# A two-layer diffusion backbone on one core: adaLN weight tiles of 256 rows by 1024 columns, later mask loads, per-feature signals, gates in the down stage

## The chip, the core and the metric

One core of a Trainium2 chip runs the whole step as one program. The metric is the device time of one execution in microseconds (us). Before the change it is 1769.07 us, the median of three runs (1765.26, 1769.07 and 1769.55 us).

## What is computed

Two groups of 128 tokens (prompt and sample, D = 1024) go through two layers. Each layer has an adaLN modulation, a mixer and a channel mixer. Layer 0 has HGRN heads beside latent attention, then a dense SwiGLU of width 2816. Layer 1 has RWKV-7 time mixing, then eight experts.

```python
def modulation(cond, w, b):
    mod = jax.nn.silu(cond) @ w + b
    return [m[:, None, :] for m in jnp.split(mod, 6, axis=-1)]
...
        sh_m, sc_m, gt_m, sh_f, sc_f, gt_f = modulation(cond, ada_w[l], ada_b[l])
        h = rms_norm(x, norm_gains[l, 0]) * (1.0 + sc_m) + sh_m
...
        x = x + gt_m * rms_norm(out, norm_gains[l, 1])
        h = rms_norm(x, norm_gains[l, 2]) * (1.0 + sc_f) + sh_f
...
        x = x + gt_f * rms_norm(ff, norm_gains[l, 3])
```

## The kernel before

Everything is written by hand, engine by engine, with semaphores; the order of instructions in each block is the order on that engine. All large weights stream through `ring`, eleven slots of 1 MB (128 partitions by 2048 floats). SyncE issues the loads in the order of use (L429 to L540) and waits for `tile_used` before it fills a slot again. Small inputs come over ScalarE's own DMA queue (L1476 to L1489), a few over GpSimd's.

**adaLN.** Twelve groups `n` (six per layer: shift, scale and gate of the mixer, and of the channel mixer) each need a product of the conditions (two columns in `CT`) with 1024 by 1024 weights. A group is four ring tiles (`ada_group`, L450). In the kernel before a tile holds 256 output columns for all 1024 rows, as 1 KB runs, so `ada_part` (L649) on TensorE waits for all four tiles before its first matmul, and `tile_freed` (L107) gives none of the four slots back before the group's end. `take_sums` (L1563) on ScalarE copies a group's sums from PSUM, `turn_mods` (L660) turns them by TensorE, and `mods` (L1961) on VectorE makes shifts and scales of them.

**The start.** TensorE waits at L695 for `rows_in` (13 loads, the two token tiles X among them) and for the constants `cst_in`, turns the parameter rows, and VectorE and ScalarE make `CT`. ScalarE squares X, takes the root and scales it (`norm_x`, L1507). TensorE does groups 0 and 1, turns the normed tokens (`turn`, L682), and VectorE and ScalarE write the modulated features `HT` (`modulated`, L1926 and L1524; eight instructions of 128 features each, one signal `ht` at the end). Then `half` (L712) multiplies HT with the 12 tiles of the input projection, interleaved with the decay levels (`level`), for which VectorE needs the masks `MSK`, cast from the load `msk` by GpSimd (L554).

**Between the output projection and the SwiGLU.** TensorE multiplies four tiles of `ev_w_out` (`tile_product`, L635), then does groups 6 and 7, turns them and waits for the normed X. ScalarE copies each tile of the output into O (`take`, L1553), then squares all of O (`norm_o`, L1519), takes groups 6 and 7, and then squares X again (`norm_x(1)`). VectorE multiplies O by the gates (`gated`), adds to X (`residual`), makes `mods` 6 and 7, scales X and modulates. After HT, TensorE spreads the gate vector of the channel mixer over the tokens (`gates(1)`, L668: 16 matmuls into banks 4 to 7), ScalarE copies it to GB, and only then `hidden()` (L922) begins. It computes the SwiGLU by a seven-product scheme: `gate_up(j)` for 11 column blocks, then `down(n)` for 11 row blocks. VectorE prepares sums of weights (`up_sums`) and of features (`x_sums`, L2235 to L2241); `gate_up(0)` needs the first features for its first product and all of `x_sums` for its second (L953 to L955).

Of the kernel before, what the change touches and what calls it, by code (L numbers as in the profile page):

```python
# [28 lines left out]
P = 128  # L29
# [75 lines left out]


def tile_freed(m):  # L107

    for n, a in enumerate(ADA_FIRST):
        if a <= m < a + ADA_TILES:  # L110
            return ada_taken(n)
    return m + 1
# [62 lines left out]
def program(nc, t, out):  # L175
    ctx = ExitStack()
    with ctx:
# [90 lines left out]

        def turned_bank(n):
            return bank[(6, 7, 7, 7, 7, 7, 6, 7, 5, 6, 7, 7)[n]]  # L270
# [12 lines left out]
        EPS1, EPS2, SQ4 = SM[:, 192:193], SM[:, 193:194], SM[:, 194:198]  # L283
        XX = O[:, :, :].rearrange("p s (c n) -> p (s c) n", n=NST * P)
# [143 lines left out]
        def _(sp):  # L428
            walk = Walk()  # L429

            def tile(parts, i=None, per=0, dues=0):

                n = walk.n
                s, _ = walk.next(len(parts))
                if i is not None:
                    sp.wait_ge(sem("tile_used"), i * per + (n - RING + 1))
                    sp.wait_ge(sem("tile_used0"), i * per + (n - RING + 1))
                elif n >= RING:
                    sp.wait_ge(sem("tile_used"), tile_freed(tile_before(n)))
                for dst, src in parts:  # L440
                    sp.dma_start(dst(ring[:, s, :]), src).then_inc(sem(f"slot{s}"), 16)
# [102 lines left out]
        def _(pool):  # L544
# [20 lines left out]
            g.memset(KR[:, 0, 0:64], 0.0).then_inc(sem("kr_zero"), 1)  # L565
            g.memset(KR[:, 1, 0:64], 0.0).then_inc(sem("kr_zero"), 1)
            g.memset(KR[:, 2, 0:64], 0.0).then_inc(sem("kr_zero"), 1)
# [17 lines left out]
            pool.wait_ge(sem("tile_used"), tile_freed(N_V - RING))  # L585
# [17 lines left out]
        def _(pe):  # L603
# [43 lines left out]
            ada_tiles = []  # L647
# [47 lines left out]
            pe.wait_ge(sem("rows_in"), 16 * 13)  # L695
            pe.wait_ge(sem("cst_in"), 16)
# [12 lines left out]
            pe.wait_ge(sem("ht"), 2)  # L709
            held = {}  # L710

            def half(p, a):  # L712

                n = TW if EVEN_ORDER[p] < 11 else 160
                if a == 0:
                    held["w"] = arrived()[:, 0:KC * n].rearrange("p (k n) -> p k n", k=KC)
                    if p >= 2:
                        pe.wait_ge(sem("proj_copied"), p - 1)
                w, b = held["w"], bank[p % 2]
# [104 lines left out]
            pe.wait_ge(sem("kr_zero"), 3)  # L824
# [97 lines left out]
            def hidden():  # L922


                def gate_up(j):
# [42 lines left out]
                def down(n):  # L968
# [23 lines left out]
                    product(3, hs(3), w[:, 1, 1, :])  # L992

# [8 lines left out]
            pe.wait_ge(sem("ht"), 4)  # L1002
            gates(1)
            pe.wait_ge(sem("gb_copied"), 8)
# [37 lines left out]
            pe.wait_ge(sem("kk2"), 1)  # L1042
            for n in range(4):
                mm(target()[:, :], blk, W[6][:, n * 512:(n + 1) * 512], start=True, stop=True).then_inc(sem("proj_done"), 1)
# [282 lines left out]
            pe.wait_ge(sem("ht"), 8)  # L1327
# [139 lines left out]
        def _(act):  # L1467
# [8 lines left out]
            load(CST[:, :], t["cst"], "cst_in")  # L1476
# [10 lines left out]
            load(X[:, 0, :], t["x_prompt"][0], "rows_in")  # L1487
            load(X[:, 1, :], t["x_sample"][0], "rows_in")
            load(W[5][:, 0:MASKS * P], t["msk"], "msk_in")  # L1489
            act.wait_ge(sem("rows_in"), 16 * 13)  # L1490
            act.wait_ge(sem("pv"), 2)
# [5 lines left out]
            def load_root():  # L1497

                act.wait_ge(sem("eps"), 2)
                A(SM[:, 198:199], EPS1, ACT.Sqrt)  # L1500
# [22 lines left out]

            def modulated(k, scale, shift):  # L1524
# [9 lines left out]
                ins.then_inc(sem("ht"), 1)  # L1534

            def copy_gates(n):
                for k in range(4):
                    act.wait_ge(sem("gb_done"), 4 * n + k + 1)
                    A(GB[:, k // 2, (k % 2) * 512:(k % 2 + 1) * 512], bank[4 + k][:, :], ACT.Copy).then_inc(sem("gb_copied"), 1)  # L1539
# [30 lines left out]

            norm_x(0)
            for n in range(2):
                take_sums(n)
            modulated(0, 0, 0)
            def take_gates(p, dst):

                proj[0] += 1
                filled(N_EVEN_IN + p)
                at = slice(dst, dst + 512)
                A(FB[0][:, at], bank[p % 2][:, :], ACT.Sigmoid)  # L1580
                A(KG[:, at], bank[p % 2][:, :], ACT.Sigmoid, scale=-1.0).then_inc(sem("proj_copied"), 1)

            def take_even(p, dst, src, func=ACT.Copy):
                proj[0] += 1
                filled(N_EVEN_IN + p)
                A(dst, src(bank[p % 2]), func).then_inc(sem("proj_copied"), 1)
# [81 lines left out]
            load_root()  # L1668
            act.wait_ge(sem("down_done"), 1)
# [5 lines left out]
            sq[0] += 1  # L1675
            act.wait_ge(sem("meansq"), 1)
            A(SM[:, 4:6], SM[:, 2:4], ACT.Sqrt, scale=1.0 / D, bias=EPS1).then_inc(sem("root"), 1)
# [231 lines left out]
        def _(dve):  # L1909
# [16 lines left out]
            def modulated(k, scale, shift):  # L1926
# [9 lines left out]
                ins.then_inc(sem("ht"), 1)  # L1936
# [11 lines left out]
            def gated(n):  # L1948

                dve.wait_ge(sem("gb_copied"), 4 * (n + 1))  # L1950
                for st in range(NST):
                    v.tensor_tensor(TO[:, st, :], O[:, st, :], GB[:, st, :], ALU.mult).then_inc(sem("gated"), 1)

# [26 lines left out]
            v.memset(EPS1, EPS).then_inc(sem("eps"), 1)  # L1980
            v.memset(EPS2, 1e-12).then_inc(sem("eps"), 1)
# [4 lines left out]
            dve.wait_ge(sem("rows_in"), 16 * 13)  # L1986
# [6 lines left out]
            dve.wait_ge(sem("msk_bytes"), 1)  # L1993
            taken = [0]
# [237 lines left out]
            dve.wait_ge(sem("ht"), 4)  # L2232
# [98 lines left out]
            dve.wait_ge(sem("ht"), 6)  # L2331
# [393 lines left out]
```

## Time and profile before

| | before |
|---|---|
| median of the runs | 1769.07 us |
| profiled execution, its own time | 1767.48 us |
| its span in the profile | 1765.7 us |
| TensorE matmul busy | 1646.2 us (93%) |
| VectorE, ScalarE, GpSimd busy | 530.8, 299.8, 16.4 us |
| mean granted clock of TensorE | 0.971 |
| moved by DMA | 408.94 MB |

The trace counts from the span's start. A matmul of 32-bit floats appears as two records of MATMUL (PE) and of weight loads (PEld), so 32 records are 16 matmuls of the program. The chain of work is followed back from the last instruction; what lies on it decided the end. The granted clock is 1.00 at 2.4 GHz and 0.50 at 1.2 GHz.

### The profile page before, as it was taken

The numbers are of one execution on the slowest core, as the hardware profiler recorded it, in microseconds if no ns is written. First come the engines' busy times: TensorE is split into PE (matmuls) and PEld (weight loads), VectorE is DVE, ScalarE is ACT, GpSimd is POOL, SyncE is SP. The second block draws the span as 40 slices with busy tenths as digits, with TensorE's granted clock in tenths as the row PEclk, the third lists the DMA queues.
The fourth block names the chain that finished last, engine by engine and source line by source line (L and its number), as shares of the span: only waits on it lengthen the run. The fifth ranks groups of instructions, "written<-read, shape, count | busy, mean of one in ns | idle before, by whom it ended". The sixth has DMA issues, their size and how long they took to land.

```text
span 1765.7 us, 59234 instructions
## 1 busy us (share of the span) xinstructions
PE 1646.2 (93%) x27345; PEld 1469.7 (83%) x27345; DVE 530.8 (30%) x1253; ACT 299.8 (17%) x684; POOL 16.4 (1%) x32
## 2 busy tenths in 40 slices
PE   3999898999979999999498999999999999999996
PEld 1888477998447889889377999999999999999995
DVE  0363425767463446665614100000000101000001
ACT  1111413011023314333213001010101000010001
POOL 1000000000000000000000000000000000000000
PEclk9999998999999999999887999999999999999998
DMA  9722697545583320000524999999999999999880
GB/s 329 256 96 79 209 293 241 189 154 190 182 260 87 131 73 5 7 5 7 171 96 176 347 344 352 384 346 371 361 350 346 348 355 352 360 357 368 334 329 25
DMA packets 212032, 408.94 MB, mean 232 GB/s; under 512 B 13090, under 2 KB 135252, under 8 KB 211796
## 3 DMA queue, kind: packets, MB, share of 16 engines
q1 hardware_dynamic: 207344, 398.91, 63.9%
q8 instruction: 215, 3.52, 0.8%
q0 software_dynamic: 1184, 3.41, 0.7%
q10 hardware_dynamic: 3268, 2.93, 0.5%
q14 instruction: 21, 0.17, 0.0%
HBM read 403.30 MB, written 1.92 MB: 229 GB/s over the span
## 4 chain that ended last, share of the span: by engine, by line
PE 46%; PEld 42%; DVE 4%; issue 3%; ACT 2%; SPq 1%; DMA 1%; DVEq 0%; PEldq 0%; POOL 0%; ACTq 0%
PEld bank L1394 26%; PEld bank L1415 13%; PE bank L945 8%; PE bank L976 4%; PE bank L631 3%; PE bank L628 3%; PE bank L722 3%; PE bank L725 2%; PE bank L1155 2%; PE bank L1115 2%; PE bank L656 2%; PE bank L747 2%; PE bank L1151 2%; PE bank L1140 2%; PE bank L1091 2%
## 5 line engine op out<-in xcount | busy, mean ns | idle before, releaser
L1394 PEld LDWEIGHTS bank<-w,ring 128*64 128x64 f32 x11264 | 468.0, 137 | 19.4 <-issue 18.4
L1394 PE MATMUL bank<-w,ring 128*64 128x96 f32 x11264 | 476.7, 246 | 3.9 <-issue 3.2
L1415 PE MATMUL bank<-w,ring 128*64 128x96 f32 x5632 | 239.0, 246 | 2.8 <-issue 2.8
L1415 PEld LDWEIGHTS bank<-w,ring 128*64 128x64 f32 x5632 | 234.2, 137 | 5.9 <-issue 4.9
L2664 DVE TENSOR_TENSOR w<-w,bank 128x384 f32<-128x384 f32 (+1 forms) x48 | 23.6, 518 | 620.9 <-PE bank L1394 620.9
L1878 ACT ACTIVATE w<-bank 128x384 f32<-128x384 f32 (+1 forms) x48 | 20.5, 462 | 460.4 <-PE bank L1394 460.3
L656 PE MATMUL bank<-ring,ct 128*32 128x256 f32 x768 | 48.3, 405 | 16.0 <-DMA ring<-in_ada_w 14.4
L628 PE MATMUL bank<-w,ring 128*128 128x256 f32 x256 | 57.6, 387 | 5.8 <-DVE w L2342 5.2
L628 PEld LDWEIGHTS bank<-w,ring 128*128 128x128 f32 x256 | 49.4, 194 | 14.0 <-DVE w L2342 5.5
L631 PE MATMUL bank<-ring,w 128*128 128x256 f32 x256 | 58.1, 391 | 0.9 <-DVE w L1942 0.9
L631 PEld LDWEIGHTS bank<-ring,w 128*128 128x128 f32 x256 | 50.2, 197 | 8.5 <-DVE w L1942 1.3
L656 PEld LDWEIGHTS bank<-ring,ct 128*32 128x32 f32 x768 | 25.4, 116 | 35.8 <-issue 20.5
L2671 DVE SCALAR_TENSOR_TENSOR o<-bank,w,o 128x512 f32<-128x512 f32 x32 | 24.0, 751 | 90.0 <-PE bank L1376 88.0
L1155 PE MATMUL bank<-ht 64*64 64x64 f32 x1280 | 49.7, 219 | 0.0
L722 PE MATMUL bank<-ht,ring 128*128 128x256 f32 x192 | 45.3, 394 | 2.2 <-ACT ht L1532 2.2
L722 PEld LDWEIGHTS bank<-ht,ring 128*128 128x128 f32 x192 | 37.0, 196 | 8.3 <-ACT ht L1532 2.4
L1155 PEld LDWEIGHTS bank<-ht 64*64 64x64 f32 x1280 | 43.3, 135 | 0.5
L945 PE MATMUL bank<-ht,ring 128*128 128x128 f32 x352 | 43.0, 275 | 0.7 <-ACT gb L1539 0.7
L945 PE MATMUL bank<-w 128*128 128x128 f32 x352 | 42.9, 275 | 0.0
L945 PE MATMUL bank<-w,ring 128*128 128x128 f32 x352 | 42.9, 275 | 0.0
L725 PE MATMUL bank<-ring,ht 128*128 128x256 f32 (+1 forms) x192 | 41.9, 371 | 0.0
L945 PEld LDWEIGHTS bank<-ht,ring 128*128 128x128 f32 x352 | 41.1, 192 | 0.9 <-ACT gb L1539 0.9
(420 smaller groups left out, 1982.7 us busy)
## 6 DMA issues: line engine op xcount, KB each, us to landing
ring<-in_moe_w_gate SPq DMA_DIRECT2D x88, 1024.0 KB, 6.3
ring<-in_moe_w_up SPq DMA_DIRECT2D x88, 1024.0 KB, 6.5
ring<-in_moe_w_down SPq DMA_DIRECT2D x88, 1024.0 KB, 6.3
ring<-in_ada_w SPq DMA_DIRECT2D x48, 1024.0 KB, 6.2
ring<-in_ev_w_in SPq DMA_DIRECT2D x11, 1024.0 KB, 12.0
ring<-in_ffn_w_gate SPq DMA_DIRECT2D x11, 1024.0 KB, 7.7
ring<-in_ffn_w_up SPq DMA_DIRECT2D x11, 1024.0 KB, 5.6
ring<-in_ffn_w_down SPq DMA_DIRECT2D x11, 1024.0 KB, 6.5
```

The lines of the kernel that those rows point to most:

```text
L628: ins = mm(b[:, a * TW:(a + 1) * TW], w[:, k, a * P:(a + 1) * P], src[:, k, :], start=k == 0, stop=k == KC - 1)
L631: ins = mm(b[:, a * TW:a * TW + n], src[:, k, a * P:(a + 1) * P], w[:, k, 0:n], start=k == 0, stop=k == KC - 1)
L656: ins = mm(sums_bank(n)[32 * j:32 * j + 32, 0:TW], CT[:, NST * k:NST * k + 32], w[:, k, :], start=k == 0, stop=k == KC - 1)
L722: ins = mm(b[:, a * TW:(a + 1) * TW], w[:, k, a * P:(a + 1) * P], HT[:, k, :], start=k == 0, stop=k == KC - 1)
L725: ins = mm(b[:, a * TW:a * TW + n], HT[:, k, a * P:(a + 1) * P], w[:, k, 0:n], start=k == 0, stop=k == KC - 1)
L747: ins = mm(bank[2 + 2 * (n % 2) + h][:, j * P:(j + 1) * P], KG[hp, seg], WQ[hp, seg] if lv else W[0][hp, qs], start=True, stop=True)
L945: ins = mm(region(j, r)[:, which * P:(which + 1) * P], lhs(which, k), rhs(k), start=first and which == 0 and k == 0, stop=k == 3, skip_gro ...
L976: ins = mm(bank[DOWN_BANK[p]][:, :], lhs, rhs, start=n == 0, stop=n == FT - 1)
L1091: ins = mm(bank[7 - n % 2][:, a * TW:(a + 1) * TW], XS["v"][:, k, a * P:(a + 1) * P], held["w"][:, k, :], start=k == 0, stop=k == KC - 1)
L1155: ins = mm(bank[2 + d][hp, (4 + j) * DH:(5 + j) * DH], IZ[hp, d, j, :], IP[i % 2][hp, d, j, :], start=True, stop=True)
L1394: ins = [mm(b[hp, (a % 4) * CAP:(a % 4 + 1) * CAP], w[:, k, a * P + hp.start:a * P + hp.stop], XG[:, kk, :], start=kk == 0 and a % 4 == 0, ...
L1415: ins = [mm(bank[4 + c // 4][hp, (c % 4) * CAP:(c % 4 + 1) * CAP], w[:, k, c * P + hp.start:c * P + hp.stop], HIDU[:, s % 2, 2 * part + k, :],
```

## The change

1. A tile of an adaLN group holds 256 rows by 1024 columns, in runs of 4 KB. TensorE uses each tile when it is there and gives its slot back at once.
2. The constants are loaded in two parts (the first 128 columns at the start), the tokens X signal `x_in` instead of `rows_in`, and the masks and the other constants are loaded on ScalarE's queue behind `norm_x(0)`.
3. `modulated` signals each feature block (`ht0` by VectorE, `ht1` by ScalarE). The first products of the input projection wait for one block at a time (they go to bank 6 instead of bank 0), and the first product of the SwiGLU waits for four blocks of the prompt.
4. The mixer's output is squared by tiles of 256 columns behind each copy, the sums of squares are added by VectorE, and O is multiplied by the gates by tiles.
5. Group 7's sums are copied by VectorE, and group 6's by ScalarE between the two squares of `norm_x(1)`.
6. `gates(1)` is no longer done ahead of the SwiGLU, but in four parts behind `down(1)` to `down(4)`, all in bank 6.

```diff
@@ sync
-                    sp.wait_ge(sem("tile_used"), tile_freed(tile_before(n)))
+                    sp.wait_ge(sem("tile_used"), tile_before(n) + 1)
...
-                    tile([cols(t["ada_w"][l], (ADA_TILES * a + j) * TW)])
+                    src = kp(t["ada_w"][l])[:, 2 * j:2 * j + 2, a * D:(a + 1) * D]
+                    tile([(lambda slot: slot.rearrange("p (k n) -> p k n", k=2), src)])
@@ tensor
             def ada_part(n, part):
-                if part == 0:
-                    ada_tiles[:] = [arrived()[:, :].rearrange("p (k n) -> p k n", k=KC) for _ in range(ADA_TILES)]
-                    if 3 <= n < 6:
-                        pe.wait_ge(sem("ada_sums"), n)
-                for k in range(4 * part, 4 * part + 4):
-                    for j, w in enumerate(ada_tiles):
-                        ins = mm(sums_bank(n)[32 * j:32 * j + 32, 0:TW], CT[:, NST * k:NST * k + 32], w[:, k, :], start=k == 0, stop=k == KC - 1)
-                        if k == KC - 1:
-                            ins.then_inc(sem("tile_used"), 1)
+                if part == 0 and 3 <= n < 6:
+                    pe.wait_ge(sem("ada_sums"), n)
+                for j in (2 * part, 2 * part + 1):
+                    w = arrived()[:, :].rearrange("p (k n) -> p k n", k=2)
+                    for k in (2 * j, 2 * j + 1):
+                        for q in range(4):
+                            ins = mm(sums_bank(n)[32 * q:32 * q + 32, 0:TW], CT[:, NST * k:NST * k + 32],
+                                     w[:, k % 2, q * TW:(q + 1) * TW], start=k == 0, stop=k == KC - 1)
+                    ins.then_inc(sem("tile_used"), 1)
...
+            def gates_part(n, part, b):
+                if part:
+                    pe.wait_ge(sem("gb_copied"), 4 * n + part)
+                st = part // 2
+                for c in range(4):
+                    ins = mm(b[:, c * P:(c + 1) * P], AGS[n // 2][:, n_gate(n), 4 * (part % 2) + c, st:st + 1].to_broadcast([P, P]),
+                             ident, start=True, stop=True)
+                ins.then_inc(sem("gb_done"), 1)
...
-            pe.wait_ge(sem("rows_in"), 16 * 13)
-            pe.wait_ge(sem("cst_in"), 16)
+            pe.wait_ge(sem("rows_in"), 16 * 12)
...
-            pe.wait_ge(sem("ht"), 2)
...
+                    if p == 0 and a == 0:
+                        pe.wait_ge(sem("ht0"), k + 1)
+                        pe.wait_ge(sem("ht1"), k + 1)
...
+                    if j == 0:
+                        pe.wait_ge(sem("ht0"), KC + 4)
                     product(0, block(0, 0), x(0, 0), True, "seven")
...
+                    if 1 <= n <= 4:
+                        gates_part(1, n - 1, bank[6])
...
             turn(token_major(O), 2)
-            pe.wait_ge(sem("ht"), 4)
-            gates(1)
-            pe.wait_ge(sem("gb_copied"), 8)
             hidden()
@@ scalar
+            act.wait_ge(sem("x_in"), 32)
             norm_x(0)
+            load(W[5][:, 0:MASKS * P], t["msk"], "msk_in")
+            load(CST[:, P:], t["cst"][:, P:], "cst_in")
...
-                take(O[:, :, n * TW:(n + 1) * TW], N_EVEN_OUT + n, src=halves)
-            act.wait_ge(sem("proj_copied"), proj[0])
-            norm_o()
-            for n in (6, 7):
-                take_sums(n)
-            norm_x(1)
+                take_out(N_EVEN_OUT, n)
+            root_of_parts(1)
+            norm_x(1, lambda: take_sums(6))
             modulated(2, 2, 1)
-            copy_gates(1)
...
             load_root()
+            copy_gates(1, [bank[6]] * 4)
@@ vector
-            dve.wait_ge(sem("proj_copied"), PROJ_ODD)
-            gated(0)
+            gated_tiles(0, PROJ_ODD)
             residual(0)
-            for n in (6, 7):
-                mods(n)
+            mods(6)
+            dve.wait_ge(sem("ada_sums"), 7)
+            dve.wait_ge(sem("tile_used"), ada_taken(7))
+            v.tensor_copy(ada_sums(7), sums_bank(7)[:, 0:TW]).then_inc(sem("ada_sums"), 1)
+            mods(7)
             normed_x()
```

The order of ScalarE's instructions at the start, before the change (`cst`, `x` and `msk` are loads on its own DMA queue, the two ACTIVATE rows of `o` are `norm_x(0)`):

```order
L1474 DMA cst<-in_cst 128x833
...
L1474 DMA x<-in_x_prompt 128x1024
L1474 DMA x<-in_x_sample 128x1024
L1474 DMA w<-in_msk 128x1536
L1492 ACT_TABLE_LOAD [waits pv]
L1492 ACTIVATE ct<-pv 128x16 [waits rows_in]
L1495 ACTIVATE o,sm<-x 128x1024 x2
```

and with the change:

```order
L1484 DMA cst<-in_cst 128x128
...
L1484 DMA x<-in_x_sample 128x1024
L1501 ACT_TABLE_LOAD [waits pv]
L1501 ACTIVATE ct<-pv 128x16 [waits rows_in]
L1504 ACTIVATE o,sm<-x 128x1024 [waits x_in]
L1504 ACTIVATE o,sm<-x 128x1024
...
L1526 ACTIVATE o<-x,sm 128x1024 [waits rs]
L1484 DMA w<-in_msk 128x1536
L1484 DMA cst<-in_cst 128x705
```

The masks and the rest of the constants have moved behind the last instruction of the norm.

TensorE between the output projection and the SwiGLU, before (L656 is `ada_part`, L665 `turn_mods`, L687 `turn`, L674 `gates`, L945 the SwiGLU's products):

```order
L631 MATMUL bank<-ring,w 128x256 x64
L656 MATMUL bank<-ring,ct 32x256 x64
L665 MATMUL bank<-cst,w 128x128 x4
L687 MATMUL bank<-cst,o 128x128 x16
L674 MATMUL bank<-cst,ag 128x128 x16
L945 MATMUL bank<-ht,ring 128x128 x8
```

and with the change, where the first six rows are the same place and the rows below the dots are in the down stage (L985):

```order
L629 MATMUL bank<-ring,w 128x256 x64
L652 MATMUL bank<-ring,ct 32x256 x64
L661 MATMUL bank<-cst,w 128x128 x4
L693 MATMUL bank<-cst,o 128x128 x16
L952 MATMUL bank<-ht,ring 128x128 x8
L952 MATMUL bank<-w 128x128 x8
...
L985 MATMUL bank<-ring,w 128x512 x2
L670 MATMUL bank<-cst,ag 128x128 x4
L985 MATMUL bank<-ring,w 128x512
```

The 16 gate matmuls have left the place ahead of the first product and stand, four by four, in the down stage.

## Rows read from the trace of the kernel before

**Rows 1.** Page, part 4: share of the chain by engine.

```profile
PE 46%; PEld 42%; DVE 4%; issue 3%; ACT 2%; SPq 1%; DMA 1%; DVEq 0%; PEldq 0%; POOL 0%; ACTq 0%
```

**Rows 2.** Waits of TensorE: who, for what, us in total, times, longest.

```profile
PE bank L697 <- DMA x<-in_x_sample: 14.8, 1, 14.8
PE bank L656 <- DMA ring<-in_ada_w: 14.4, 2, 8.3
```

**Rows 3.** The chain at the start: start us, us, what.

```profile
21.70 14.11 DMA ring<-in_ada_w
...
35.94 5.65 PE bank L656 x64
...
43.45 2.92 ACT ht L1532 x8
...
46.41 19.22 PE bank L722 x80
...
71.47 3.65 PE bank L722 x16
```

**Rows 4.** Stretches: length, busy by engine, granted clock, DMA share, GB/s.

```profile
0.00:3.00 3.00, 0.00 (x0) 0.00 (x0) 0.15 (x3) 0.00 (x0) 0.20 (x4) 1.00 0.38 83
3.00:35.80 32.80, 6.65 (x67) 3.46 (x67) 1.36 (x3) 6.69 (x10) 7.43 (x13) 0.96 1.08 347
36.00:69.00 33.00, 30.61 (x191) 24.27 (x192) 5.15 (x14) 6.26 (x13) 0.00 (x0) 0.89 1.10 349
931.00:937.00 6.00, 4.07 (x18) 3.70 (x18) 3.66 (x13) 3.68 (x9) 0.00 (x0) 0.50 1.02 418
33.00:39.00 6.00, 3.06 (x32) 1.68 (x36) 0.00 (x0) 0.00 (x0) 0.00 (x0) 0.50 1.10 349
```

**Rows 5.** Timeline at the start: start us, us, instruction [idle before, releaser].

```profile
17.18 1.46 POOL L554 CAST msk<-w 128x1536 uint8<-128x1536 f32 x1 [16.76 <-DMA w<-in_msk]
21.86 1.15 ACT L1517 ACTIVATE o<-x,sm 128x1024 f32<-128x1024 f32 x1 [0.34 <-DVE sm L1918]
...
42.32 1.91 PE L687 MATMUL bank<-cst,o 128*128 128x128 f32 x16
...
63.41 0.69 DVE L2003 TENSOR_TENSOR w<-w 128x512 f32<-128x512 f32 x1 [17.69 <-ACT w L1581]
```

**Rows 6.** The chain around the SwiGLU's start: start us, us, what.

```profile
240.11 4.14 PE bank L674 x32
...
271.87 7.17 PE bank L656 x128
...
283.44 3.66 PE bank L687 x16
...
288.68 5.59 PE bank L674 x32
...
294.95 137.84 PE bank L945 x1232
432.79 66.09 PE bank L976 x154
```

**Rows 7.** Timeline of the same place.

```profile
279.06 0.38 ACT L1568 ACTIVATE w<-bank 128x256 f32<-128x256 f32 x1 [3.07 <-PE bank L656]
...
280.25 0.17 DVE L1976 SCALAR_TENSOR_TENSOR ag<-ag,pv 128x16 f32<-128x16 f32 x1
...
281.95 0.17 DVE L1918 RECIPROCAL sm<-sm 128x2 f32<-128x2 f32 x1 [1.52 <-ACT sm L1505]
...
288.66 0.69 DVE L2235 TENSOR_TENSOR w<-ht 128x512 f32<-128x512 f32 x1 [0.80 <-ACT ht L1532]
...
291.68 0.68 DVE L2241 TENSOR_TENSOR w<-ht,w 128x512 f32<-128x512 f32 x1
...
296.84 1.95 PE L945 MATMUL bank<-w 128*128 128x128 f32 x16
```

**Rows 8.** Granted clock from 290 us on (columns as in rows 4).

```profile
290.00:294.00 4.00, 4.00 (x28) 4.00 (x27) 3.57 (x6) 1.79 (x3) 0.00 (x0) 0.70 1.10 348
```

More of the change, by code:

```diff
@@ L104, in ada_taken @@
     return ADA_FIRST[n] + ADA_TILES
[L107 to L112, printed above, removed]
 def moe_tiles():
@@ L267, in sums_bank, with even_bank @@
             return bank[(4, 5, 6, 6, 6, 6, 4, 5, 0, 1, 4, 6)[n]]
+        def even_bank(p):
+            return bank[p % 2] if p else bank[6]
         def turned_bank(n):
@@ L283, in program @@
         EPS1, EPS2, SQ4 = SM[:, 192:193], SM[:, 193:194], SM[:, 194:198]
+        SQ8 = SM[:, 8:16].rearrange("p (s n) -> p s n", s=NST)
         XX = O[:, :, :].rearrange("p s (c n) -> p (s c) n", n=NST * P)
@@ L564, in _ @@
                     load(S0A[64 * h:64 * h + 64, d, :, 64 * h:64 * h + 64], states[h], "s0_in")
-            g.memset(KR[:, 0, 0:64], 0.0).then_inc(sem("kr_zero"), 1)
-            g.memset(KR[:, 1, 0:64], 0.0).then_inc(sem("kr_zero"), 1)
-            g.memset(KR[:, 2, 0:64], 0.0).then_inc(sem("kr_zero"), 1)
+            g.memset(KR[:, 0, 0:64], 0.0).then_inc(made("pool_chain"), 1)
+            g.memset(KR[:, 1, 0:64], 0.0).then_inc(made("pool_chain"), 1)
+            g.memset(KR[:, 2, 0:64], 0.0).then_inc(made("pool_chain"), 1)
             pool.wait_ge(sem("ckn"), 2)
@@ L718, in half @@
                         pe.wait_ge(sem("proj_copied"), p - 1)
-                w, b = held["w"], bank[p % 2]
+                w, b = held["w"], even_bank(p)
                 for k in range(KC):
+                    if p == 0 and a == 0:
+                        pe.wait_ge(sem("ht0"), k + 1)
+                        pe.wait_ge(sem("ht1"), k + 1)
                     if p < 6:
@@ L823, in _ @@
                 ins.then_inc(sem("heads_done"), 1)
-            pe.wait_ge(sem("kr_zero"), 3)
+            pe.wait_ge(sem("pool_chain"), 4)
             pe.wait_ge(sem("kr"), 2)
@@ L1042, in _ @@
             pe.wait_ge(sem("kk2"), 1)
+            pe.wait_ge(sem("cst_in"), 16)
             for n in range(4):
@@ L1326, in _ @@
             turn_mods(11)
-            pe.wait_ge(sem("ht"), 8)
+            pe.wait_ge(sem("ht0"), 4 * KC)
+            pe.wait_ge(sem("ht1"), 4 * KC)
             w = arrived()[:, 0:KC * NE].rearrange("p (k n) -> p k n", k=KC)
@@ L1486, in _ @@
             load(rows[2][48:50, :], r8(t["mla_q_norm"][0]), "rows_in")
[L1487 to L1491, printed above, removed]
+            load(X[:, 0, :], t["x_prompt"][0], "x_in")
+            load(X[:, 1, :], t["x_sample"][0], "x_in")
+            act.wait_ge(sem("rows_in"), 16 * 12)
+            act.wait_ge(sem("pv"), 4)
             A(CT[:, 0:KC * NST].rearrange("p (k s) -> p k s", s=NST), PV[:, COND:COND + 16].rearrange("p (s k) -> p k s", k=KC), ACT.Silu).then_inc(sem("ct"), 1)
@@ L1497, in load_root @@
             def load_root():
-                act.wait_ge(sem("eps"), 2)
+                act.wait_ge(sem("pv"), 4)
                 A(SM[:, 198:199], EPS1, ACT.Sqrt)
@@ L1522, in norm_o, with take_out, root_of_parts @@
                 root()
+            def take_out(tile, n):
+                take(O[:, :, n * TW:(n + 1) * TW], tile + n, src=halves)
+                act.wait_ge(sem("proj_copied"), proj[0])
+                for st in range(NST):
+                    A(W[9][:, st * TW:(st + 1) * TW], O[:, st, n * TW:(n + 1) * TW], ACT.Square,
+                      accum_out=SQ8[:, st, n:n + 1]).then_inc(sem("out_squares"), 1)
+            def root_of_parts(n):
+                sq[0] += 1
+                act.wait_ge(sem("meansq"), n)
+                A(SM[:, 4:6], SM[:, 2:4], ACT.Sqrt, scale=1.0 / D, bias=EPS1).then_inc(sem("root"), 1)
             def modulated(k, scale, shift):
@@ L1952, in gated, with gated_tiles @@
                     v.tensor_tensor(TO[:, st, :], O[:, st, :], GB[:, st, :], ALU.mult).then_inc(sem("gated"), 1)
+            def gated_tiles(n, copied):
+                dve.wait_ge(sem("gb_copied"), 4 * (n + 1))
+                for c in range(4):
+                    at = slice(c * TW, (c + 1) * TW)
+                    dve.wait_ge(sem("proj_copied"), copied - 3 + c)
+                    ins = v.tensor_tensor(TO[:, :, at], O[:, :, at], GB[:, :, at], ALU.mult)
+                    if c >= 2:
+                        ins.then_inc(sem("gated"), 1)
+                dve.wait_ge(sem("out_squares"), 4 * n + 8)
+                v.tensor_reduce(SM[:, 2:4], SQ8, AX.X, ALU.add).then_inc(sem("meansq"), 1)
             def residual(n):
@@ L1978, in mods @@
                     dve.wait_ge(sem("mod"), so_far("mod"))
-            v.memset(EPS1, EPS).then_inc(sem("eps"), 1)
-            v.memset(EPS2, 1e-12).then_inc(sem("eps"), 1)
+            v.memset(EPS1, EPS).then_inc(made("pv"), 1)
+            v.memset(EPS2, 1e-12).then_inc(made("pv"), 1)
             v.memset(CT[:, KC * NST:], 0.0).then_inc(made("pv"), 1)
@@ L1985, in _ @@
             dve.wait_ge(sem("pv"), so_far("pv"))
-            dve.wait_ge(sem("rows_in"), 16 * 13)
+            dve.wait_ge(sem("x_in"), 32)
             normed_x()
@@ L1993, in _ @@
             dve.wait_ge(sem("msk_bytes"), 1)
+            dve.wait_ge(sem("cst_in"), 16)
             taken = [0]
@@ L2231, in _ @@
             modulated(2, 2, 1)
-            dve.wait_ge(sem("ht"), 4)
+            dve.wait_ge(sem("ht0"), 2 * KC)
+            dve.wait_ge(sem("ht1"), 2 * KC)
             x = lambda half, st: HT[:, 4 * half:4 * half + 4, st * P:(st + 1) * P]
@@ L2329, in _ @@
             modulated(3, 0, 0)
-            dve.wait_ge(sem("ht"), 6)
+            dve.wait_ge(sem("ht0"), 3 * KC)
+            dve.wait_ge(sem("ht1"), 3 * KC)
             h16, x16 = (b.rearrange("p (g n) -> p g n", n=P) for b in (HTf, Of))
```

23 lines of the change are left out of this document (10 added, 13 removed).

## The prediction

> **What bounds the kernel now.** I read the page's shares of the chain first [rows 1]: matmuls and weight loads of TensorE hold 88% of it. So time can only be won where the chain leaves TensorE or where TensorE runs slowly, and work added to TensorE costs its full length. The list of TensorE's waits comes next [rows 2]: the two large waits on loads, 14.8 and 14.4 us, are both in the first 36 us. The chain there [rows 3] shows the last adaLN tile of group 1 issued at 21.70 and landed at 35.80. Then all 64 records of group 1 run in 5.65 us, and the input projection starts at 46.41, when the last feature is there. From then on the chain shows matmuls only, through the whole input projection, so a start that is earlier by some microseconds should arrive at the end whole. The second place is the stretch before the SwiGLU [rows 6]: groups 6 and 7 end at 271.87 + 7.17 = 279.04, the turn starts at 283.44, the gates at 288.68, the SwiGLU at 294.95. After that, TensorE is busy without a hole through both stages of the SwiGLU.
>
> **The start, up to the last adaLN tile.** The DMA engines are full from 3 us on [rows 4]. By the windows, 0.25 MB had moved by 3.0 and 32.8 x 0.347 = 11.38 MB more by 35.8, so the tile landed behind 11.6 MB. With the change, what lies ahead of it? The eight tiles, the tokens and the parameter rows remain. The masks (0.79 MB) and the later part of the constants (0.36 MB) are issued behind `norm_x(0)`, whose last instruction began at 21.86 and lasted 1.15 [rows 5]. ScalarE no longer waits for X to make `CT`, and X has fewer bytes ahead of it, so I put this issue at 19 to 21 us. That is well before the last tile lands, on a queue that shares the engines. So I count these 1.15 MB as still ahead of the tile: the deferral itself wins little. GpSimd's loads (0.44 MB, behind the masks' cast at 17.18 [rows 5]) now fall behind the tile. That leaves 11.2 MB.
>
> The rate is the open price. Full engines moved 349 GB/s with runs of 1 KB and 418 GB/s with the experts' runs of 4 KB [rows 4]. After the change all adaLN tiles have 4 KB, but the rows, the masks in between and the instruction loads do not, so I take 385, the middle: 3.0 + (11.2 - 0.25) / 0.385 = 31.4 us. At 349 it is 34.4, at 418 it is 29.2, and if the masks were not ahead of it 28.5. Term: **-4.4 us** (-1.4 to -7.3). The Trainium skill, page "DMA: Bandwidth & Descriptors", section "Where 436 GB/s comes from", says that loads from HBM are bound at about 358 GB/s per core; by that rule the longer runs would win hardly anything and the term would be the small one. The trace disagrees with it at 418 GB/s over 6 us, so it is a rival only.
>
> **Behind the last tile.** The 64 records of group 1 ran from 35.94 to 41.59, for the most part at the low clock (0.50 from 33 to 39 [rows 4]). Now the first three tiles are done before the fourth lands, and 16 records remain, four steps of four at 0.43 us each (the low clock), 1.7 us. Before, 5.8 us from landing to the end; now 1.9. Term: **-3.9 us**. From there to the first projection matmul it took 46.41 - 41.59 = 4.8 us. Of this the copy of the sums and their turn took some 0.6, and the 16 records of turned tokens 1.91 [rows 5]; the rest was the wait for the last of eight modulated blocks (ScalarE, 43.45 + 2.92). With a signal per block, the projection starts behind the turn. But TensorE now works in short pieces before it, so the turn may run at the low clock, 3.66 instead of 1.91, as at 283.44 [rows 6]. Taking 2.8 for it, I get 3.4 instead of 4.8, -1.4. The first five halves took 19.22 us where later ones take 3.65 each, 18.25 in all [rows 3]; without the hole before them I give half of that excess back, -0.5. Term: **-1.9 us** (-1.0 to -3.2). Costs that I set at nothing: the extra signals (on instructions that are there anyway), and the late masks, since VectorE's first instruction behind them began at 63.41 [rows 5] and they should be bytes by 30. Were that cover gone, the third rival below is the price.
>
> Sum of the start: **-10.2 us** (-6.3 to -14.4).
>
> **Before and in the SwiGLU.** The tiled squares and gates finish the output norm about 0.6 us earlier, which is not on the chain: `norm_x(1)` was held by group 7 at 279.06 [rows 7]. Now it is not held, but the reciprocal that its scaling needs stands on VectorE behind `mods(7)`, and this behind VectorE's own copy of group 7. The copy (0.4, as ScalarE's 0.38), the turn and the two small instructions bring this to about 281.1; it was 281.95. So X, the turn and the last feature come 0.9 to 1.1 earlier, at 287.6 instead of 288.64. The first product starts behind the turn, at about 286.1. Then `x_sums` is late next: from the first sum at 288.66 to the end of the last at 292.36 took 3.7 us [rows 7], and this was hidden by the gates. It isn't now. 287.6 + 3.7 = 291.3 for the second product, where before it began at 296.84 [rows 7]: **-5.5 us**.
>
> Against it stand 32 records of gates in the down stage, where TensorE is the bound. They took 4.14 at 240.11 [rows 6]; the same shape inside the SwiGLU costs 137.84 / 1232 = 0.112 each [rows 6], 3.6 in all. I take **+3.6** (to +4.1), since they stand between warm matmuls. ScalarE's copies there hold nothing: the next part comes a whole row block (66.09 / 11 = 6.0 us [rows 6]) later. Last, the clock. Before, the gates were what ran at the low level (5.59 instead of 4.14; 0.70 granted from 290 to 294 [rows 8]) and the SwiGLU began at full speed. Now the SwiGLU's first products stand there, with a wait of about 3 us behind the first. Low-clock time costs half of itself: **+0.9** (0 to +2.5). Sum: **-1.0 us** (-1.9 to +1.1).
>
> **All terms:** -10.2 - 1.0 = -11.2 us. Against the profiled execution, 1767.48 us, this is 1756.3; the median shown stands 1.6 above that execution, so I forecast **1757.9 us**. The other edits (slots given back by tile, group 8 to 11 tiles) I cost at nothing: TensorE waits for no adaLN tile but at the start [rows 2], and the experts follow the same instructions as before.
>
> **Rivals.**
> 1. The long runs are not faster here (the skill's bound, or the parameter rows and masks dilute them): tile at 34.4, total -8.2, **1760.9 us**. For it: 349 to 1 KB runs was steady for 33 us. Against it: 418 at 931 us. Chance 0.12.
> 2. The win at the SwiGLU turns over and the start gives a part back. The mechanism is the clock: after the bursts at the start, the whole turn runs low (3.66, not 2.8: +0.9) and so does the first half of the projection (3.65 more, and the 0.5 that I gave back), and the SwiGLU's start loses 2.5 instead of 0.9. Total -11.2 + 6.7 = -4.5, **1764.6 us**. For it: the level fell to 0.50 in holes of 3 us before. Against it: TensorE has no hole once group 1's last tile is there. Chance 0.10.
> 3. The masks starve, and it gets slower. ScalarE's queue would get the engines only when SyncE's stream is dry. By the old rate the stream behind the tile is 12.2 MB, 35 us, so it ends at 31.4 + 35 = 66.3. With 2 for landing and GpSimd's 1.46 for the cast [rows 5] VectorE could start at 69.8 instead of 63.4 - 10.2 = 53.2: +16.6, in all 1757.9 + 16.6 = **1774.5 us**. The point at which it decides: masks as bytes later than 53 us. Against it: before, masks and X together came through by 16.76 [rows 5] while SyncE's queue was as full. The Trainium skill, same page, section "Queues, rings and completion order", says that each engine goes round robin between queues; by that rule this can't happen, and the arrival at 16.76 agrees. Chance 0.04.
>
> **How the numbers follow.** My forecast's case has 0.74, of which a tenth or so falls short of the threshold. A difference under 0.3% (5.3 us) cannot be told from none here, so faster means under 1763.8. Faster gets 0.67 + 0.12 + some 0.03 of rival 2, that is 0.82; same 0.13; slower (over 1774.4) 0.05. The range goes from 1752.5 (start -14.4 and a little from the SwiGLU) to 1764.5, which takes in rival 1 and the bounds of the terms, and leaves out rival 3 and the worse half of rival 2.
>
> **What would show it.** Right: the last tile of group 1 lands at 29 to 34 us with the engines at 370 to 418 GB/s before it; 16 records behind it; the first projection matmul at 36 to 37 us; TensorE unbroken from there; the second product 5 us earlier relative to the end of the output projection, with a hole of 2 to 3 us before it that ends with `x_sums`; the down stage 3.6 us longer. Wrong: a projection that starts later than 40 us, VectorE waiting for the masks, or a clock below 1.00 for more than 5 us behind 290.

## The result, and the profile after

The changed kernel takes 1754.8 us (median of 4 runs, 1752.05 to 1756.52), the kernel before 1769.31 us beside it: a ratio of 0.9927, with a 95% interval of 0.991 to 0.9945. It is 14.5 us faster; 1757.9 us was forecast, with a range of 1752.5 to 1764.5. The profiled execution took 1756.52 us (span 1754.7), the slowest of the four. All ratios are of fast executions; one execution of the kernel called "masks first, small loads late" below took 3933.15 us and is left out.

The chain of the changed kernel at its start (start us, us, what), which answers to [rows 3]:

```profile
5.95 24.74 DMA ring<-in_ada_w
...
30.73 1.93 PE bank L652 x16
32.66 1.19 PE bank L661 x4
33.86 2.00 PE bank L693 x16
35.86 17.33 PE bank L729 x80
```

The last tile of group 1 lands at 30.69 instead of 35.81, 16 records follow it instead of 64, and the projection's first matmul (35.86) stands right behind the turn; before it was at 46.41, behind ScalarE's last feature block. The first five halves (80 records) take 17.33 us, where [rows 3] has 19.22. The stretches of the changed kernel, with the columns of [rows 4]:

```profile
3.00:30.69 27.69, 10.27 (x115) 4.59 (x115) 1.36 (x3) 6.68 (x10) 0.25 (x1) 0.94 1.02 400
12.00:27.00 15.00, 10.27 (x115) 4.59 (x115) 1.36 (x3) 6.68 (x10) 0.00 (x0) 1.00 1.02 409
36.00:60.00 24.00, 24.00 (x133) 20.66 (x132) 4.22 (x10) 6.04 (x12) 2.17 (x7) 1.00 1.10 340
```

The same full engines move 409 GB/s with runs of 4 KB and 340 with the 1 KB runs of the input projection's tiles. The timeline of the changed kernel shows where the masks went:

```profile
21.48 0.33 ACTq L1484 DMA_DIRECT2D w<-in_msk  x1
...
30.44 1.46 POOL L552 CAST msk<-w 128x1536 uint8<-128x1536 f32 x1 [30.01 <-DMA w<-in_msk]
...
50.99 0.69 DVE L2037 TENSOR_TENSOR w<-w 128x512 f32<-128x512 f32 x1 [13.66 <-ACT w L1606]
```

They are issued at 21.48 and land at 30.01, just ahead of the last adaLN tile, and are bytes 19 us before VectorE's first instruction behind them; its wait ends with ScalarE, not with the masks.

The chain before the SwiGLU answers to [rows 6]:

```profile
259.45 7.04 PE bank L652 x128
...
268.48 0.18 DVE sm L1938
...
269.98 1.95 PE bank L693 x8
...
272.02 3.01 ACT ht L1554 x8
...
275.12 0.69 DVE w L2272
...
277.01 1.20 DVE ring L2242 x2
278.22 0.62 DVE w L2278
278.83 0.14 issue
278.97 21.07 PE bank L952 x172
```

What the gates used to hide is now on the chain: ScalarE's features, then VectorE's sums of features, up to the second product at 278.97. Of these 3.7 us, 1.20 (L2242) are no sum of features but two sums of weights, which stand in VectorE's order between the third and the fourth feature sum. TensorE in the timeline there:

```profile
273.31 1.98 PE L952 MATMUL bank<-ht,ring 128*128 128x128 f32 x16
...
278.97 2.80 PE L952 MATMUL bank<-w 128*128 128x128 f32 x16 [3.68 <-DVE w L2278]
...
281.56 2.84 PE L952 MATMUL bank<-w,ring 128*128 128x128 f32 x16
...
284.24 1.95 PE L952 MATMUL bank<-w 128*128 128x128 f32 x16
```

Behind a hole of 3.68 us the next two products take 2.80 and 2.84 instead of 1.95. The granted clock from 279 to 283 us is 0.63:

```profile
279.00:283.00 4.00, 4.00 (x23) 4.00 (x24) 2.21 (x5) 0.00 (x0) 0.00 (x0) 0.63 1.10 348
```

The gates in the down stage cost what the SwiGLU's records cost, four times 0.89:

```profile
428.64 0.89 PE bank L670 x8
429.53 6.01 PE bank L985 x14
435.54 0.89 PE bank L670 x8
```

### The profile page after: what moved, and what is told of

The parts are those of the page before. It is cut to its first block, busy times and chain, and to the rows that moved or that the text cites. A ratio compares the mean times of both kernels' runs of the same rounds, so it can differ in the third digit from the quotient of the medians.

```text
span 1754.7 us, 59240 instructions
## 1 busy us (share of the span) xinstructions
PE 1646.6 (94%) x27345; PEld 1469.8 (84%) x27345; DVE 532.1 (30%) x1257; ACT 300.5 (17%) x695; POOL 16.4 (1%) x32
## 4 chain that ended last, share of the span: by engine, by line
PE 46%; PEld 43%; DVE 4%; issue 3%; ACT 2%; DMA 1%; SPq 0%; DVEq 0%; PEldq 0%; POOL 0%; ACTq 0%
PEld bank L1404 27%; PEld bank L1425 13%; PE bank L952 8%; PE bank L985 4%; PE bank L629 3%; PE bank L626 3%; PE bank L729 2%; PE bank L732 2%; PE bank L1164 2%; PE bank L1124 2%; PE bank L754 2%; PE bank L1160 2%; PE bank L1100 2%; PE bank L1149 2%; PE bank L652 2%
## 5 line engine op out<-in xcount | busy, mean ns | idle before, releaser
L626 PEld LDWEIGHTS bank<-w,ring 128*128 128x128 f32 x256 | 49.5, 194 | 14.2 <-DVE w L2380 5.6
L952 PEld LDWEIGHTS bank<-w 128*128 128x128 f32 x352 | 41.7, 195 | 3.8 <-DVE ring L2242 3.8
L985 PE MATMUL bank<-ring,w 128*128 128x512 f32 x88 | 42.2, 592 | 0.0
L952 PEld LDWEIGHTS bank<-w,ring 128*128 128x128 f32 x352 | 42.1, 196 | 0.0
```

The source lines that it names most:

```text
L952: ins = mm(region(j, r)[:, which * P:(which + 1) * P], lhs(which, k), rhs(k), start=first and which == 0 and k == 0, stop=k == 3, skip_gro ...
L985: ins = mm(bank[DOWN_BANK[p]][:, :], lhs, rhs, start=n == 0, stop=n == FT - 1)
```

## The experiments

The 95% interval of a ratio is 0.35 to 0.7% wide here (6 to 13 us), more than most of the parts. So each kernel is read by its profile in stretches. "Landing" is the last tile of group 1, "projection" the first matmul of the input projection, then come the time from there to the output projection, from the end of group 7 to the first matmul of the k projection in layer 1 (the SwiGLU and both its ends), and the rest. From the output projection to the end of group 7 it took 34.80 us in the kernel before and 34.66 or 34.67 in all others. A ratio is to the kernel before, run beside it.

| kernel | landing | projection | to output proj. | group 7 to k proj. | rest | ratio to before (95%) |
|---|---|---|---|---|---|---|
| before | 35.81 | 46.41 | 197.83 | 242.52 | 1244.1 | |
| changed | 30.69 | 35.86 | 195.96 | 242.45 | 1245.8 | 0.9927 (0.991 to 0.9945) |
| changed, again | 30.89 | 35.95 | 195.95 | 242.41 | 1244.4 | 0.9913 (0.9893 to 0.9933) |
| gates ahead | 30.86 | 36.77 | 193.08 | 239.82 | 1247.2 | 0.9918 (0.9889 to 0.9947) |
| old tiles | 34.52 | 43.65 | 194.70 | 241.85 | 1247.4 | 0.9977 (0.9957 to 0.9997) |
| masks first | 33.75 | 39.24 | 194.31 | 241.91 | 1243.7 | 0.9949 (0.9929 to 0.997) |
| masks first, small loads late | 31.53 | 37.02 | 194.30 | 241.90 | 1244.3 | 0.9935 (0.9915 to 0.9956) |
| masks last | 28.71 | 34.32 | 194.31 | 241.80 | 1243.4 | 0.9927 (0.9898 to 0.9956) |
| all features | 30.87 | 38.92 | 196.04 | 242.33 | 1244.8 | 0.9946 (0.9925 to 0.9966) |
| three sums | 31.07 | 36.93 | 193.09 | 239.11 | 1243.3 | 0.9904 (0.9868 to 0.9939) |
| gates in the hole | 31.23 | 37.65 | 194.67 | 239.54 | 1246.0 | 0.9903 (0.9885 to 0.9921) |
| masks last, gates ahead | 28.81 | 34.67 | 193.08 | 239.81 | 1244.5 | 0.9893 (0.9875 to 0.9911) |
| masks last, hole, three sums | 28.80 | 34.47 | 193.14 | 238.19 | 1248.5 | 0.9879 (0.9858 to 0.990) |

These groups shared a chip: gates ahead, old tiles, masks first and masks last; then changed again, gates in the hole and the two combinations; then the other three.

How much is scatter? Six profiles have the same program up to the projection but for one wait (changed twice, gates ahead, three sums, gates in the hole, and all features up to its wait). They land between 30.69 and 31.23, and the five without the longer wait have the projection 5.06 to 6.42 us behind it, by the level of the clock in the turn. So single differences below half a microsecond at the landing, and below 1.4 us behind it, show nothing.

**The changed kernel again.**

> The changed kernel once more, as a yardstick for the kernels beside it on the same chip: 1754 to 1757 us. Its profile shows how much of a difference is chance. Theory of the clock (the low-clock pieces ahead of the SwiGLU are set by what TensorE did there and come again): the second product starts 12.5 us behind the end of group 7 and at the low level again, with 1.7 us lost in the first SwiGLU stage. Rival (they fall by chance): this profile differs from the first by 1.5 us or more in that stretch.

The landings differ by 0.2 us. From the projection's start to the k projection (508.94 and 508.97 us) the two profiles agree within 0.1 us, the low-clock pieces included: the second product starts 12.4 us behind group 7 and the two products take 2.84 and 2.80. So the theory held, in these two executions. The rest, which is the same program in all kernels but before and old tiles, scatters from 1243.3 to 1248.5. That is the limit of what a single execution tells.

**Old tiles.**

```diff
-                    src = kp(t["ada_w"][l])[:, 2 * j:2 * j + 2, a * D:(a + 1) * D]
-                    tile([(lambda slot: slot.rearrange("p (k n) -> p k n", k=2), src)])
+                    tile([cols(t["ada_w"][l], (ADA_TILES * a + j) * TW)])
```

(with `ada_part` and `tile_freed` as before the change, and the adaLN groups later in the kernel too)

> The changed kernel with adaLN tiles of 1024 rows by 256 columns and slots given back by group, everything else as changed. Theory (the tile's shape carries most of the start): the last tile of group 1 lands at 34 to 35 us instead of 30.7, 64 records behind it instead of 16, first projection matmul at 42 to 43.5 us instead of 35.9, so 6.5 to 7.5 us slower than the changed kernel. Rival (the later masks carry the earlier landing): it lands by 32 us and the loss is 4 us or less.

```profile
34.65 6.36 PE bank L661 x64
...
43.65 6.54 PE bank L738 x30
```

The landing is 3.8 us later and the projection 7.8 us later; the loss at the projection is slightly above what was expected. The engines were full and moved 354 GB/s up to the landing, where the changed kernel has 400, and that makes most of the 3.8. Not all of it has to be the tile's shape: in this kernel the masks land at 25.46, so GpSimd issues its small loads from 27.30 on, ahead of the landing again. But from 12 to 27 us, before them, it was already 366 against 409. The other 4 us are the 48 records that stand behind the landing again, and the clock. At the k projection 5.9 us of the loss are left (514.87 against 508.94), of the 12.6 that the change wins there.

**Masks first, and small loads late.** The first puts the two loads right behind X:

```diff
             load(X[:, 1, :], t["x_sample"][0], "x_in")
+            load(W[5][:, 0:MASKS * P], t["msk"], "msk_in")
+            load(CST[:, P:], t["cst"][:, P:], "cst_in")
...
             norm_x(0)
-            load(W[5][:, 0:MASKS * P], t["msk"], "msk_in")
-            load(CST[:, P:], t["cst"][:, P:], "cst_in")
```

> The changed kernel with the masks and the later constants loaded right behind the tokens X, not behind the norm. Theory (in the changed kernel they still pass ahead of the last adaLN tile, so their place wins nothing): the last tile lands at 30.5 to 31.5 us, the whole within 1 us of the changed kernel; GpSimd's small loads move ahead of the tile and may cost up to 1 us. Rival (the deferral wins bytes): landing at 33 us or later, 2.8 us slower.

The rival's number came, 33.75, though at the k projection only 1.2 us of the loss are left (510.13 against 508.94). But was it for the rival's reason? In this kernel GpSimd's loads also move forward, since GpSimd waits for the masks. Its stretches:

```profile
3.00:33.75 30.75, 11.47 (x115) 4.78 (x115) 1.66 (x3) 6.69 (x10) 7.48 (x13) 0.90 1.03 384
27.00:33.75 6.75, 1.93 (x16) 0.59 (x16) 0.00 (x0) 0.00 (x0) 1.31 (x5) 0.55 1.04 321
```

By the landing it had moved 30.75 x 0.384 = 11.8 MB, the changed kernel 27.69 x 0.400 = 11.1; and the last 6.75 us ran at 321 GB/s. So the second kernel holds back the small loads alone:

```diff
+            pool.wait_ge(sem("tile_used"), 2 * ADA_TILES)
             load(HG, t["hgrn_norm"][0].partition_broadcast(P), "extras_in")
```

> The kernel with the masks first again, but GpSimd issues its small loads (0.44 MB, the states in runs of 256 bytes) only when TensorE has used all eight adaLN tiles. Theory from the runs before (the place of the masks counts only because the small loads follow them; ahead of the last tile they cost 3 us, by bytes and by short runs): the last tile lands at 30.5 to 31 us as in the changed kernel, where masks first alone gave 33.75. Rival (the masks themselves cost it): 33 us or later again.

```profile
31.53 0.04 issue
31.57 1.94 PE bank L653 x16
```

It lands at 31.53: 2.2 of the 3.1 us were the small loads. The theory had allowed 31 at most; but against the 30.69 to 31.23 of the profiles with the changed kernel's start only 0.3 to 0.8 us stay with the masks' own place, hardly more than the scatter. That the masks do delay the tile, wherever they stand ahead of it, is shown by the next kernel.

**Masks last.** The two loads move behind `take_sums(1)`.

> The changed kernel with the masks and the later constants issued only once the sums of group 1 are copied. Theory (1.15 MB at 410 GB/s leave the path of the last adaLN tile): it lands 2.8 us earlier, near 27.9 us, the masks are bytes by 45 us, before VectorE wants them near 50, and the whole is 2 to 3 us faster than the changed kernel. Rival (the bytes ahead don't matter, or the masks become late): same time, or VectorE waits for the masks and it is slower.

```profile
5.87 22.84 DMA ring<-in_ada_w
...
34.32 5.68 PE bank L729 x26
```

It lands at 28.71, and at 28.81 and 28.80 in the two combinations below: about 2 us earlier and not 2.8. The cast is done at 39.2 (37.76 + 1.47), and VectorE's first instruction behind it begins at 49.46, again behind ScalarE. The projection is 1.5 us earlier, and the k projection 3.9 us (505.09), of which 2.3 come from the two stretches between, by the clock. In the ratio (0.9927, as the changed kernel) the gain does not show.

**All features.** The first projection matmul waits for `ht0` and `ht1` at 8.

> The changed kernel, in which the first projection matmul waits for all eight feature blocks of both halves. Theory: the wait ends with ScalarE's last block, 2 us after the turn, so the first projection matmul stands 7.3 to 7.5 us behind the landing instead of 5.2, and the output projection follows 2 us later, or more where the clock falls in the hole. Rival (the features are out of the way, since the turn sets the start): under 0.7 us.

```profile
33.83 3.40 PE L693 MATMUL bank<-cst,o 128*128 128x128 f32 x16
...
38.92 9.30 PE L729 MATMUL bank<-ht,ring 128*128 128x256 f32 x42 [1.69 <-ACT ht L1554]
```

8.05 us from landing to the projection instead of 5.17. Of these 2.9 us the wait is 1.7. The rest is a turn that ran at the low level (3.40 us for 16 records; 2.21 in the changed kernel, read from the same view); it stands ahead of the wait, so it is not its doing. The output projection follows 3.1 us later, more than the 2 us of the theory, by the same slow turn. Only the wait at the input projection is tried here, not the one at the SwiGLU.

**Gates ahead.** Wait for HT, `gates(1)`, its copies and the wait for them stand where they were before the change; the four parts are out of `down`.

> The changed kernel, with the 16 gate matmuls and their copies back between the features and the SwiGLU, as before. Theory (the move of the gates is worth little: a later second product is paid for by the gates in the down stage and by products at the low clock): the profiles differ only there; the second product starts about 5.5 us later counted from the end of the output projection, the first SwiGLU stage is 1.5 us shorter, the down stage 3.6 us shorter, and the whole is within 1 us of the changed kernel. Rival (moving the gates carries a part of the win): 3 to 5 us slower.

Neither came. The stretch from group 7 to the k projection is 2.6 us *shorter* than in the changed kernel (239.82 against 242.45). (The stretch up to the output projection is 2.9 us shorter as well, with the same instructions; more on this below.) Its chain:

```profile
269.88 2.56 DVE ht L1956 x8
272.44 0.81 issue
273.26 3.82 PE bank L680 x32
...
277.10 0.61 ACT gb L1563
...
277.75 7.30 PE bank L952 x63
```

The gates took 3.82 us here, not the 5.59 of [rows 6]. So its first product comes 277.75 - 264.52 = 13.2 us behind group 7 and its second 1.8 later, at 15.0, where the changed kernel has it at 12.5: the move wins 2.5 us there, not 5.5. Against it stand 3.6 in the down stage and 1.7 lost at the low clock.

**Masks last, gates ahead** repeats it beside the changed kernel.

> Masks last, and the gates ahead of the SwiGLU as before the change. Theory from the first four runs (moving the gates is a wash or a small loss, masks last win 2 to 3 us): 2 to 4 us faster than the changed kernel. Rival (the kernel with the gates ahead was only lucky with the clock): equal to masks last alone within 1 us, and so 2 to 3 us faster than the changed kernel; the two stretches, up to the output projection and from there to the k projection, tell which.

239.81 again, with all times 2 us earlier than in the kernel above. The gates took 3.82 again. Five kernels with the gates in `down` and the full hole, apart from the changed kernel's two profiles, have 241.80 to 242.33. So this is no luck of one execution. The rival of this run, that it would equal masks last alone, did not come: masks last alone (241.80) is 2.0 us longer there. The median is 5.3 us under the changed kernel's beside it (1749.20 against 1754.52), more than the theory gave.

**Gates in the hole.** The hole is TensorE's wait between the first and the second product. Parts 0 and 1 go there, into banks 5 and 6, and ScalarE copies them behind its first copy of the SwiGLU (not shown).

```diff
                     product(0, block(0, 0), x(0, 0), True, "seven")
+                    if j == 0:
+                        for part in range(2):
+                            gates_part(1, part, bank[5 + part])
...
-                    if 1 <= n <= 4:
-                        gates_part(1, n - 1, bank[6])
+                    if 1 <= n <= 2:
+                        gates_part(1, n + 1, bank[6])
```

> The changed kernel with the first two of the four gate parts put into TensorE's hole between the first and the second product of the SwiGLU (banks 5 and 6), the other two behind down(1) and down(2). Theory (the hole is free time, 3.7 us wide, and a busy TensorE keeps its clock): the down stage is 1.8 us shorter than in the changed kernel, the products behind the hole run at full speed (1.7 us won back), in all 2 to 3.5 us faster than the changed kernel. Rival (the gates run slowly and hold up the second product): no gain.

```profile
276.83 1.95 PE L670 MATMUL bank<-cst,ag 128*128 128x128 f32 x16
...
279.62 2.02 PE L952 MATMUL bank<-w 128*128 128x128 f32 x16 [0.83 <-DVE w L2285]
281.48 1.95 PE L952 MATMUL bank<-w,ring 128*128 128x128 f32 x16
```

The hole is 0.83 us wide, the products behind it run at full speed, and the stretch is 2.9 us shorter than in the changed kernel, as expected. Against "gates ahead" (239.82) it is 0.3 us.

**Three sums.** The second product uses only `x_sum(1)`, the third of the four sums that VectorE makes.

```diff
-                    pe.wait_ge(sem("x_sums"), 4)
+                    pe.wait_ge(sem("x_sums"), 4 if j else 3)
...
+                    if j == 0:
+                        pe.wait_ge(sem("x_sums"), 4)
                     product(4, block(1, 1), x_sum(3), True, "seven")
```

> The changed kernel, in which the second product of the SwiGLU waits for three of the four feature sums, the fourth being waited for ahead of the product that uses it. Theory: the second product starts with the end of the third sum, 1.8 us earlier (10.6 instead of 12.4 us behind the end of group 7), and the hole of 3.7 us shrinks to 1.9, so the clock falls less: 1.8 to 3 us faster. Rival (the third product and VectorE's weight sums are then late): under 1 us.

```profile
275.45 2.02 PE L952 MATMUL bank<-w 128*128 128x128 f32 x16 [1.90 <-DVE w L2277]
...
277.31 1.95 PE L952 MATMUL bank<-w,ring 128*128 128x128 f32 x16
```

The second product starts 10.8 us behind group 7, behind a hole of 1.90 and with no slow products: the stretch is 3.3 us shorter, slightly more than expected. Of it 1.7 is the earlier start and the rest the clock.

**Masks last, hole, three sums.**

> Masks last, two gate parts in the hole, and the second product of the SwiGLU waits for three of the four feature sums (the fourth is waited for by the product that uses it). Theory: masks last win 2.8, the second product starts 1.8 earlier and the gates in the hole give 1.8 to 3.5, part of which overlap: 5 to 7 us faster than the changed kernel, near 1749. Rival (the pieces compete for the same hole): 3 to 4 us, as masks last and one of the two.

It has the lowest median and ratio: 1748.89 us (5 runs), 0.9879 of the kernel before and 5.6 us under the changed kernel's median beside it, as the theory said. Its interval overlaps those of three sums, of gates in the hole and of masks last with the gates ahead, so its place before these is not shown by the times. The stretch around the SwiGLU is the shortest of all, 238.19. The pieces overlap there, as the rival said: hole alone -2.9, three sums alone -3.3, both -4.2.

## Why the prediction was right, and where it was not

**The landing** (-4.4, came -5.1). The counted bytes were right: 27.69 x 0.400 + 0.18 gives 11.3 MB, with 11.2 forecast, and the masks were ahead of the tile as said. The rate was off: 400 rather than 385. I had counted the masks among the loads that slow it, but they are 1536 floats for each partition, runs of 6 KB; the short runs that are left weigh less than I gave them. The bound of rival 1 did not show: 409 GB/s over 15 us. The Trainium skill, page "DMA: Bandwidth & Descriptors", section "Where 436 GB/s comes from", has about 358 GB/s per core for loads from HBM; the measurement decides against it for this kernel, which runs on one core.

**The deferral of the masks** was said to win little by itself. Right for the masks' own place, 0.3 to 0.8 us, but the deferral also pushes GpSimd's loads behind the tile. I had counted their 0.44 MB (1.1 us) and not that the engines move less with them (321 GB/s in the last 6.75 us, against 380 in the last 4.5 us without them); together 2.2. Whether their short runs make it slow was not tried.

**Behind the tile** (-3.9, came 5.78 -> 1.97, -3.8) and **features** (-1.9, came -3.5, outside the term's own range of -1.0 to -3.2). Of the second term, -1.4 up to the projection came as -1.6; "all features" puts the signals themselves at 1.7 us. The rest was mis-sized. For the first five halves I compared 19.22 us with five times 3.65, saw 0.97 too much and gave back half. But 3.65 is a half that stands alone between decay levels; five in a row take 17.33, so 1.89 us were lost in the kernel before, and all of it is gone. They were lost to the clock, which was below 1.00 in the kernel before behind the hole that ends at 46.41 (0.57 from 46.4 to 50.4 us) and is 1.00 in the changed kernel from 36 us on:

```profile
45.00:48.00 3.00, 1.59 (x4) 1.33 (x5) 0.71 (x3) 1.36 (x4) 0.00 (x0) 0.77 1.10 348
48.00:55.00 7.00, 7.00 (x29) 5.96 (x29) 0.00 (x0) 0.00 (x0) 0.00 (x0) 0.86 1.10 348
```

**The sum of the start** was -10.2. It came as -5.1 - 3.8 - 1.6 - 1.9 = -12.4: the projection is 10.55 us earlier, the output projection 12.42 (244.24 to 231.82). Behind the first halves the two kernels run alike; the chain of the one follows that of the other by 12.4 us, piece by piece, up to the output projection. Both have the same low clock just ahead of it. That it need not be there shows in "gates ahead", whose stretch of 193.08 us has the same instructions. The turn and the gates of layer 0 in the changed kernel, and then in "gates ahead":

```profile
223.95 3.68 PE bank L693 x16
227.62 4.20 PE bank L680 x32
```

```profile
224.31 1.97 PE bank L693 x16
226.28 3.57 PE bank L680 x32
```

These two rows hold 2.3 of the 2.9 us between the two kernels (granted clock from 224 to 228 us: 0.50 and 1.00). TensorE's waits for VectorE's `w` from 215 to 245 us sum to 1.7 us in both. Why the level falls in one and not in the other was not found out.

**At the SwiGLU** (-1.0, came -0.1 in the profile). The second product moved from 17.8 us behind group 7 to 12.5, -5.3 (-5.5 forecast). In it, the reciprocal went from 2.91 us behind group 7 to 1.99, and the last feature from 9.60 to 8.54, both as forecast; this fits the tiled squares and the copy by VectorE, but no run leaves these out. The gates in the down stage cost 3.57 (3.6). What failed is the clock term: +0.9 was forecast, for a hole of 2 to 3 us, and 1.7 came, behind one of 3.68. And behind it the baseline: I took the 5.59 us of the gates in the kernel before as what goes away with the move. In both kernels with this start and the gates ahead they took 3.82. (Even the 4.14 at layer 0, my price at full speed, was partly low; there it is 3.57 above.) My terms put the move itself, without the earlier features, at about nothing; measured against "gates ahead" it is a loss of 2.6 us. It was hidden by the low clock of the one profile that I had. The kernel before and the changed one come out equal in this stretch because each has its slow piece there.

**The end.** The profiles differ by 11.0 us, the medians by 14.5. Up to the k projection it is 12.6 in the profiles. The rest is 1.6 us longer in the changed kernel's profile, within its scatter; whether the change moves anything there stays open. That the profiles' 11.0 meets the forecast's 11.2 so closely is luck: the start won 2.2 us more than forecast, the SwiGLU 0.9 less, and the scatter of the rest took back the remainder.

Rival 3, masks that starve, was ruled out: even the masks issued last were bytes 10 us before their use. Rival 2 had the right mechanism, a clock that falls in the hole, but of its 6.7 us only 0.8 came, at the SwiGLU.

## What to carry to other kernels

Where the chain begins with a landing, count the bytes in front of it, the length of their runs, and the work that can only begin when all is there; cutting the tile along the contraction made each piece usable by itself and made the runs longer too. Before moving work off the chain, ask what it has been covering: here the sums of VectorE came out from under the gates. The move alone lost 2.6 us; only with the hole filled with a part of the work, or with one sum less to wait for, does it come out ahead of leaving the gates in place, by 0.3 and 0.7 us, and by 1.6 with both. A stretch with a low clock in one profile is no baseline: look at a second kernel with other timing before you price a gain there.

## What the runs showed that was not expected

The clock of a stretch is not set by its instructions alone: the same instructions from the input to the output projection took 193.1 us in four kernels, 194.3 to 194.7 in four, and 196.0 in three profiles, while the same kernel gave 195.96 and 195.95 in two executions. And 0.44 MB of small loads on GpSimd's queue, with runs of 256 bytes among them, delayed a stream of 1 MB tiles by 2.2 us, twice their 1.1 us by bytes at 400 GB/s (one profile each, with landings that scatter by 0.5 us).
